# The gate norm's statistics: ten single operations in the first ten attention pairs, or two groups of five in pairs 13 and 14

## The chip, the cores and the metric

The kernel runs on one core of one Trainium2 chip. The metric is the device time of one execution in microseconds, lower is better. The profile is one further execution taken with the hardware profiler, and all times in this text are microseconds from the start of its span unless marked otherwise.

## What is computed

Two layers of a streaming encoder. 512 prompt frames (four tiles of 128 rows) and 8 x 16 new frames of running streams (a fifth tile) go through each layer:

```
xn = RMSNorm(x);  [q|k|v|q_idx|k_idx|w_idx|u|v_s|g_a|g_b] = xn @ W_in
a  = sparse attention: an indexer scores the keys, the best 128 (prompt) or 68 (streams) are kept
s  = gelu(u) * (tril(w_s) @ layer_norm(gelu(v_s)) + b_s)          the spatial gate
h  = x + (sigmoid(g_a) * (a @ W_pa) + sigmoid(g_b) * (s @ W_pb)) @ W_out
y  = h + HierMoE(RMSNorm(h))                                      top group, then two experts
```

The change concerns the `layer_norm` inside `s`, called the gate norm here: per row, the mean and the variance over 512 columns, for five tiles. The outputs of the operator depend on it only through the spatial gate and one returned tensor of normalised rows.

## The kernel before

Every engine has its own program, written out by hand, and the engines meet at semaphores. The part in question is the attention stage of each layer, between the projections of q, k, v, u and those of the two gates. It runs over 20 **pairs** (`NAP`): pairs 0 to 15 are four per prompt tile (`TILE_OF[p]` is `p // 4`), pairs 16 to 19 belong to the streams. A pair is two heads. For pair p:

- PE writes `logits(p)` two pairs ahead (lines 909 to 917), then `probs_transposes(p)` (L929), then a third of a left-over projection of u, `fill(p)` (L776, pairs 0 to 14), then `values(p-1)` (L942 for prompt tiles, L953 and L964 for streams). Before the logits of pair 16, PE waits for `stream_scores`.
- DVE runs, in iteration p of its loop (lines 1700 to 1712): `roots(p)` (the reciprocal L1663, and for the streams the two products L1668, whose two tensor inputs both lie in SBUF); `masked_logits(p+1)` (two L1650 from PSUM, then the small `tensor_scalar` L1658, which makes the exponent's bias of pair p+1 and releases ACT); the selection rounds that `ROUNDS` gives to this iteration (MAX8, MATCH_REPLACE8, L1441; the last ones are in iteration 13, after which `stream_scores` is raised); and, for p below 10, one step of the gate norm's statistics.
- ACT runs `probs_out(p-1)` (L1299), `normalise(p)` (L1289) and `exps(p+1)` (L1283); L1283 waits for L1658 of its pair, L1289 for the `roots` of its pair.

The gate norm itself has three parts. Its statistics are ten DVE operations, `ln_step(0)` to `ln_step(9)` (lines 1628 to 1638): `bn_stats` (L1634) and `bn_aggr` (L1636) for each of the five tiles, each waited for before DVE goes on, since all tiles share one small buffer; the last raises `ln_stat`. POOL waits for `ln_stat`, forms the inverse roots (L539, L542) and normalises in place: five `tensor_scalar` (L636), then ten `tensor_tensor` (L640, five products with the gain and five sums with the bias), one after the other, all 128x512 in SBUF. Each raises `ln_done`. PE's `gating(t)` (L987) waits for `ln_done`; it comes after PE has left the pairs and done its first gate projection, sixteen matmuls of L743. The SP queue waits for the last `ln_done` before it loads the weights of the second half of the gate (a load that also waits for `gating`), and POOL sends the normalised rows out (L643), raises `rows_sent`, and loads the router's weights (lines 648 to 650) after it.

Of the kernel before, what the change touches and what calls it, by code (L numbers as in the profile page):

```python
# [25 lines left out]
NT = PT + 1  # L26
# [98 lines left out]
def prior(name, L):  # L125

    return L * PER_LAYER[name]


SG_BANK = (5, 6, 7, 2, 3)  # L130
PBUF = 4
LBANK = (0, 1, 5, 6)

PROMPT_UNITS = [(t, j, g) for t in range(PT) for j in range(GQ) for g in range(KV)]
# [17 lines left out]
def build(nc, a, o):  # L152
    ctx = ExitStack()
    with ctx:
# [39 lines left out]
        rs_wide = stat[:, 110:110 + NT * (XW - D)].rearrange("p (t c) -> p t c", t=NT)  # L194
        mx, nmx, den, rden = (stat[:, 60 + PBUF * i:60 + PBUF * (i + 1)] for i in range(4))
        moments = stat[:, 18:28].rearrange("p (t c) -> p t c", c=2)
# [25 lines left out]
        q_rep = [scr[:, 512 * g:512 * g + 512] for g in range(KV)]  # L222
        probs = [scr[:, 512 * i:512 * i + 512] for i in range(PBUF)]

        probs_t = [ring[:, VCU % SLOTS, 2048 + 512 * i:2560 + 512 * i] for i in range(PBUF)]
        relu_b = [scr[:, 512 * i:512 * i + 512] for i in range(4)]
# [483 lines left out]
        def _(pe):  # L710
# [22 lines left out]
            for L in range(DEPTH):  # L733
# [168 lines left out]
                def logits(p):  # L902
# [5 lines left out]
                    for n in (2 * p, 2 * p + 1):  # L908
                        t, j, g = ATT_UNITS[n]
                        out = banks[LBANK[n % 4]][:, 0:KEYS[t]]  # L910
                        if t < PT:
# [7 lines left out]
                def probs_transposes(p):  # L919
                    if p == 0:  # L920
                        pe.wait_ge(qts_done, prior("qts_done", L) + 2)
                    for n in (2 * p, 2 * p + 1):
# [5 lines left out]
                        for i, c in enumerate(blocks):  # L928
                            mm = pe.transpose(banks[2 + n % 2][:, i * P:(i + 1) * P],  # L929
                                              probs[n % PBUF][:, c * P:(c + 1) * P], idm)  # L930
                        mm.then_inc(pt_psum, 1)

                def values(p):
# [4 lines left out]
                    if t < PT:  # L938
                        for c in range(t + 1):
                            for h in range(KV):  # L940
                                r = slice(HD * h, HD * h + HD)
                                mm = pe.matmul(banks[4][r, j * P:(j + 1) * P], qkv[:, c, V0 + HD * h:V0 + HD * h + HD],  # L942
                                               probs_t[(2 * p + h) % PBUF][:, c * P:(c + 1) * P],
                                               start=(c == 0), stop=(c == t))
                    else:
# [4 lines left out]
                        for h in range(KV):  # L950
                            r = slice(HD * h, HD * h + HD)
                            o4 = banks[4][r, :].rearrange("p (j q) -> p j q", j=GQ)
                            pe.matmul(o4[:, :, rows], qkv[:, PT, V0 + HD * h:V0 + HD * h + HD],  # L953
                                      probs_t[(2 * p + h) % PBUF][:, 2 * P:3 * P].rearrange("p (j x) -> p j x", j=GQ),
                                      start=True, stop=False)
# [437 lines left out]
        def _(dve):  # L1393
# [3 lines left out]
            def then(ins):  # L1397

                count[0] += 1
                ins.then_inc(dve_chain, 1)  # L1400
                dve.wait_ge(dve_chain, count[0])
# [171 lines left out]
            for L in range(DEPTH):  # L1573
# [47 lines left out]
                def select(t, p):  # L1621

                    begin, rounds = ROUNDS[t]
                    if begin <= p < begin + len(rounds):
                        for r in range(sum(rounds[:p - begin]), sum(rounds[:p - begin + 1])):
                            select_round(t, r)

                def ln_step(i):

                    t, what = divmod(i, 2)  # L1630
                    if i == 0:
                        dve.wait_ge(proj_free, prior("proj_free", L) + 4 * NT)
                    if what == 0:
                        then(V.bn_stats(bns, uv[:, 1, t, :]))  # L1634
                    else:
                        then(V.bn_aggr(moments[:, t, :], bns))  # L1636
                    if i == 2 * NT - 1:
                        V.nop().then_inc(ln_stat, 1)

                def masked_logits(p):  # L1640
                    t, k = TILE_OF[p], 2 * p % PBUF
                    if p and TILE_OF[p - 1] != t:
                        dve.wait_ge(dve_chain, last[t])
                    for h in range(2):
                        n = 2 * p + h
                        dve.wait_ge(s_psum, prior("s_psum", L) + n + 1)
                        if n >= PBUF:
                            dve.wait_ge(pt_psum, prior("pt_psum", L) + n - PBUF + 1)
                        raw = banks[LBANK[n % 4]][:, 0:KEYS[t]]
                        ins = V.tensor_tensor_reduce(out=probs[k + h][:, 0:KEYS[t]], in0=raw,  # L1650
                                                     in1=score(t) if t < PT else zero[:, :].broadcast_to([P, KEYS[PT]]),
                                                     scale=1.0, scalar=NEG, op0=ALU.add, op1=ALU.max,
                                                     accum_out=mx[:, k + h:k + h + 1])
                        if h == 0:
                            ins.then_inc(dve_chain, 1)
                            count[0] += 1
                    then(ins)
                    V.tensor_scalar(nmx[:, k:k + 2], mx[:, k:k + 2], -ATT_SCALE, None, ALU.mult).then_inc(p_raw, 1)  # L1658

                def roots(p):  # L1660
                    t, k = TILE_OF[p], 2 * p % PBUF
                    dve.wait_ge(p_exp, prior("p_exp", L) + 2 * p + 2)
                    ins = V.reciprocal(rden[:, k:k + 2], den[:, k:k + 2])  # L1663
                    if t == PT:

                        then(ins)
                        for h in range(2):
                            ins = V.scalar_tensor_tensor(probs[k + h][:, 3 * P:4 * P].rearrange("p (b i) -> p b i", b=STREAMS),  # L1668
                                                         over(probs[k + h][:, PAST:PAST + FRAMES], STREAMS, 1, [P, STREAMS, FRAMES]),
                                                         rden[:, k + h:k + h + 1],  # L1670
                                                         own_of[:, ATT_UNITS[2 * p + h][1], :].unsqueeze(2).broadcast_to([P, STREAMS, FRAMES]),
                                                         ALU.mult, ALU.mult)
                    ins.then_inc(rden_ready, 1)
# [26 lines left out]
                for p in range(NAP):  # L1700
                    roots(p)
                    if p + 1 < NAP:
                        masked_logits(p + 1)
                    for t in (2, 3, PT):
                        select(t, p)
                    if p == ROUNDS[PT][0] + len(ROUNDS[PT][1]) - 1:
                        dve.wait_ge(dve_chain, last[PT])
                        V.nop().then_inc(stream_scores, 1)
                    if p < 2 * NT:
                        ln_step(p)  # L1710

                for t in range(NT):
                    dve.wait_ge(u_ready, prior("u_ready", L) + t + 1)
# [138 lines left out]
```

## Time and profile before

| | |
|---|---|
| median of 3 runs | 1474.03 us (1470.98 to 1478.52) |
| the profiled execution | 1474.07 us, its span 1472.3 us, mean granted TensorE clock 0.952 |
| PE busy | 1313.5 us, 89% of the span |
| weight loads (PEld) | 727.1 us, 49% |
| DVE busy | 535.8 us, 36% |
| ACT busy | 341.9 us, 23% |
| POOL busy | 222.1 us, 15% |
| chain that ended last | PE 78%, DVE 5%, DMA 5%, issue 4%, ACT 4% |

How to read it: the shares are means over stages with different limits, so the stage of the pairs has to be read by itself, 156 to 257 in the first layer and 872 to 973 in the second. In a timeline a row is the start, the duration, the engine, the line, the operation, output and input with their sizes, how many were merged, and in brackets the idle time before it with what ended it. "Layer 0" and "layer 1" are the first and the second layer.

### The profile page before, as it was taken

What the parts mean: (1) busy time and instruction counts of PE and PEld (TensorE: products, weight loads), DVE (VectorE), ACT (ScalarE), POOL (GpSimd) and SP (SyncE); (2) the same over time, 40 slices, a digit from 0 to 9 for tenths busy, and PEclk for the clock granted to TensorE, in tenths of its full rate; (3) what the DMA queues carried; (4) which work ended last, traced back from release to release, by engine and by line L of the source; (5) the groups of instructions that cost most, each with busy time, mean ns of one, the idle gap of its engine ahead of it and who ended that gap; (6) DMA issues with size and microseconds to landing.
All of it is one profiled execution on the core that took longest, in us unless ns stands there. A gap on an engine that the chain in (4) does not pass through costs nothing.

```text
span 1472.3 us, 15258 instructions
## 1 busy us (share of the span) xinstructions
PE 1313.5 (89%) x5660; PEld 727.1 (49%) x5660; DVE 535.8 (36%) x1502; ACT 341.9 (23%) x773; POOL 222.1 (15%) x304
## 2 busy tenths in 40 slices
PE   7999898999999995988599999899999999879780
PEld 5654345544444454555475544564444445445550
DVE  1278885110111136222335779631101113442115
ACT  2232466100001100222214236541000020112121
POOL 5011033000000001223231200600000000022313
PEclk9999999999999996999799999999999999979895
DMA  8302102503304315899662210051060060369966
GB/s 236 114 13 59 58 1 70 171 1 103 111 0 167 119 51 204 342 405 374 232 150 66 63 57 1 22 180 40 0 214 1 27 244 29 140 244 409 401 230 236
DMA packets 95483, 205.61 MB, mean 140 GB/s; under 512 B 26464, under 2 KB 35904, under 8 KB 95408
## 3 DMA queue, kind: packets, MB, share of 16 engines
q1 hardware_dynamic: 80800, 178.13, 34.2%
q0 software_dynamic: 14608, 26.49, 5.1%
q8 instruction: 46, 0.75, 0.2%
q14 instruction: 29, 0.24, 0.0%
HBM read 196.29 MB, written 27.78 MB: 152 GB/s over the span
## 4 chain that ended last, share of the span: by engine, by line
PE 78%; DVE 5%; DMA 5%; issue 4%; ACT 4%; PEld 1%; PEldq 1%; POOL 1%; SPq 0%; POOLq 0%; ACTq 0%; DVEq 0%
PE bank L743 34%; PE bank L1025 9%; PE bank L1060 9%; PE bank L1106 6%; DMA uv<-xd,mb 3%; PE bank L1117 3%; PE bank L776 3%; PE bank L1093 2%; PE bank L825 1%; DVE stat L1658 1%; PE bank L1042 1%; PE bank L729 1%; PE bank L929 1%; PE bank L829 1%; PE bank L1101 1%
## 5 line engine op out<-in xcount | busy, mean ns | idle before, releaser
L743 PE MATMUL bank<-ring,xt 128*128 128x512 f32 (+1 forms) x1120 | 433.4, 544 | 8.3 <-DMA ring<-in_w_in 5.5
L743 PEld LDWEIGHTS bank<-ring,xt 128*128 128x128 f32 x1120 | 214.2, 194 | 209.5 <-issue 189.2
L1727 DVE TENSOR_TENSOR scr<-scr,bank 128x512 f32<-128x512 f32 x20 | 13.7, 687 | 368.6 <-PE bank L1025 368.6
L1060 PE MATMUL bank<-ring,xt 128*128 128x512 f32 x320 | 141.0, 595 | 0.0
L539 POOL TENSOR_SCALAR stat<-stat 128x1 f32<-128x1 f32 (+1 forms) x27 | 11.3, 418 | 802.8 <-ACT uv L1193 614.3
L1337 ACT ACTIVATE scr<-bank,stat 128x512 f32<-128x512 f32 x40 | 25.3, 683 | 347.9 <-PE bank L743 347.9
L1060 PEld LDWEIGHTS bank<-ring,xt 128*128 128x128 f32 x320 | 59.5, 191 | 67.8 <-issue 67.8
L776 PE MATMUL bank<-ring,xt 128*128 128x512 f32 x160 | 75.4, 605 | 0.0
L1025 PE MATMUL bank<-ring,att 128*128 128x512 f32 x160 | 72.5, 596 | 2.2 <-ACT sgt L1329 1.8
L1025 PE MATMUL bank<-ring,sgt 128*128 128x512 f32 x160 | 71.9, 593 | 0.0
L743 PE MATMUL bank<-more,xt 128*128 128x512 f32 x160 | 70.3, 593 | 0.0
L1762 DVE TENSOR_TENSOR xt<-bank,gain 128x512 f32<-128x512 f32 x68 | 43.8, 686 | 65.8 <-PE bank L1093 65.7
L1106 PE MATMUL bank<-ring,xt 128*64 128x256 f32 x480 | 66.1, 382 | 0.3 <-issue 0.3
L1441 DVE MAX8 stat<-mb 128x8 f32<-128x256 f32 (+3 forms) x114 | 61.6, 540 | 3.0
L1769 DVE SCALAR_TENSOR_TENSOR xt<-bank,uv,xt 128x128 f32<-128x128 f32 x34 | 11.9, 351 | 134.9 <-ACT xt L1358 134.9
L1441 DVE MATCH_REPLACE8 mb<-stat,mb 128x256 f32<-128x256 f32 (+3 forms) x114 | 59.7, 524 | 0.0
L674 POOL DMA_INDIRECT yd<-scr,mb x34 | 34.1, 1002 | 168.4 <-ACT scr L1367 162.7
L1093 PE MATMUL bank<-ident,uv 128*128 128x128 f32 x272 | 41.6, 300 | 18.9 <-DMA uv<-xd,mb 18.9
L1093 PEld LDWEIGHTS bank<-ident,uv 128*128 128x128 f32 x272 | 35.0, 196 | 43.5 <-issue 32.3
L1025 PEld LDWEIGHTS bank<-ring,att 128*128 128x128 f32 x160 | 30.0, 190 | 41.3 <-issue 39.1
L929 PE MATMUL bank<-ident,scr 128*128 128x128 f32 x208 | 35.1, 293 | 16.4 <-ACT scr L1289 16.4
L743 PEld LDWEIGHTS bank<-more,xt 128*128 128x128 f32 x160 | 30.4, 190 | 38.2 <-issue 38.2
(285 smaller groups left out, 1810.0 us busy)
## 6 DMA issues: line engine op xcount, KB each, us to landing
ring<-in_w_in SPq DMA_DIRECT2D x12, 2048.0 KB, 9.2
ring<-in_w_ed SPq DMA_DIRECT2D x32, 512.0 KB, 18.1
ring<-in_w_eg SPq DMA_DIRECT2D x26, 512.0 KB, 10.0
ring<-in_w_eu SPq DMA_DIRECT2D x26, 512.0 KB, 17.1
ring<-in_w_out SPq DMA_DIRECT2D x4, 2048.0 KB, 12.4
more<-in_w_ed SPq DMA_DIRECT2D x14, 512.0 KB, 11.2
qkv<-in_w_eg SPq DMA_DIRECT2D x12, 512.0 KB, 6.7
qkv<-in_w_eu SPq DMA_DIRECT2D x12, 512.0 KB, 8.1
```

What stands on the lines that cost most here:

```text
L674: pool.indirect_dma_start(out=yd, in_=yout[z], in_offset=None, out_offset=bass.IndirectOffsetOnAxis(ap=index(b, 1, q), axis=0), bounds_che ...
L743: mm = pe.matmul(out, xt[:, k, t * P:(t + 1) * P], rhs[:, k, :], start=(k == 0), stop=(k == KD - 1))
L776: mm = pe.matmul(banks[7][:, :], xt[:, k, t * P:(t + 1) * P], rhs[:, k, :], start=(k == 0), stop=(k == KD - 1))
L929: mm = pe.transpose(banks[2 + n % 2][:, i * P:(i + 1) * P], probs[n % PBUF][:, c * P:(c + 1) * P], idm)
L1025: mm = pe.matmul(b[2 + half_][:, :], src[:, j, t * P:(t + 1) * P], w[:, 4 * half_ + j, :], start=(j == 0), stop=(j == 3))
L1060: mm = pe.matmul(banks[5 + n % 3][:, :], xt[:, k, t * P:(t + 1) * P], w[:, k, :], start=(k == 0), stop=(k == KD - 1))
L1093: mm = pe.transpose(banks[first + k // 4][:, (k % 4) * P:(k % 4 + 1) * P], xin[q][:, k:D:KD], idm)
L1106: mm = pe.matmul(banks[2 + z][BR * h:BR * h + BR, 0:2 * P].rearrange("p (m f) -> p m f", m=2), xin_t[z][:, k, BR * h:BR * h + BR], w[:, :, ...
L1117: mm = pe.matmul(banks[4 + c][BR * h:BR * h + BR, :], hidden_t[z][:, BR * h:BR * h + BR], two[h][1][c] if two[h] is places[PLACES - 1] els ...
L1337: ins = act.activation(scr[:, c0:c0 + 512], banks[4 * (n % 2) + m][:, :], ACT.Sigmoid, scale=rs1[:, n % NT:n % NT + 1])
L1441: make(*args, **kwargs).then_inc(dve_chain, 1)
L1762: V.tensor_tensor(xin_t[z][:, 4 * hf:4 * hf + 4, :], banks[first + hf][:, :].rearrange("p (k r) -> p k r", k=4), gain[:, L, 1, 4 * hf:4 * ...
```

## The change

The ten statistics operations are no longer spread one to an iteration over DVE's iterations 0 to 9. The first five (`bn_stats`, `bn_aggr`, `bn_stats`, `bn_aggr`, `bn_stats`) stand at the end of iteration 13, behind the last selection round and behind the raise of `stream_scores`, and the other five at the end of iteration 14, with the raise of `ln_stat` behind the last. What each operation does, and everything on POOL, PE, ACT and SP, is as it was.

```diff
 PBUF = 4
+LN_AT = (13, 14)
 LBANK = (0, 1, 5, 6)
...
                     if p == ROUNDS[PT][0] + len(ROUNDS[PT][1]) - 1:
                         dve.wait_ge(dve_chain, last[PT])
                         V.nop().then_inc(stream_scores, 1)
-                    if p < 2 * NT:
-                        ln_step(p)
+                    if p in LN_AT:
+                        for i in range(NT):
+                            ln_step(NT * LN_AT.index(p) + i)
```

## Rows read from the trace of the kernel before

**Rows 1.** The chain that ended last, both layers: start, us, what.

```profile
221.16 9.83 DVE stat L1658
...
256.56 7.11 PE bank L743 x16
...
935.98 9.30 DVE stat L1658
...
972.52 7.11 PE bank L743 x16
```

**Rows 2.** Timeline of POOL, the gate norm, layers 0 and 1.

```profile
208.36 10.32 POOL L636 TENSOR_SCALAR uv<-uv,stat 128x512 f32<-128x512 f32 x5
218.66 12.31 POOL L640 TENSOR_TENSOR uv<-uv,ring 128x512 f32<-128x512 f32 x10
...
932.95 12.31 POOL L640 TENSOR_TENSOR uv<-uv,ring 128x512 f32<-128x512 f32 x10
```

**Rows 3.** Timeline of DVE, statistics and the operations beside POOL's work, layer 0.

```profile
163.89 0.68 DVE L1634 BATCH_NORM_STATS2 stat<-uv 128x6 f32<-128x512 f32 x1
...
206.35 0.17 DVE L1636 BATCH_NORM_AGGREGATE stat<-stat 128x2 f32<-128x6 f32 x1
...
215.00 0.33 DVE L1658 TENSOR_SCALAR stat<-stat 128x2 f32<-128x2 f32 x1
...
219.81 0.69 DVE L1650 CUSTOM_DVE_ANT_0 scr<-bank,mb 128x512 f32<-128x512 f32 x1
```

**Rows 4.** Timeline of DVE, pairs 15 to 19, layer 0.

```profile
234.04 0.17 DVE L1658 TENSOR_SCALAR stat<-stat 128x2 f32<-128x2 f32 x1
...
244.29 0.61 DVE L1668 SCALAR_TENSOR_TENSOR scr<-scr,stat,own_of 128x128 f32<-128x128 f32 x2
...
245.69 0.17 DVE L1658 TENSOR_SCALAR stat<-stat 128x2 f32<-128x2 f32 x1
...
249.56 0.61 DVE L1668 SCALAR_TENSOR_TENSOR scr<-scr,stat,own_of 128x128 f32<-128x128 f32 x2
...
250.93 0.17 DVE L1658 TENSOR_SCALAR stat<-stat 128x2 f32<-128x2 f32 x1
```

**Rows 5.** Timeline of ACT around the long wait and in pair 18, layer 0.

```profile
223.89 1.34 ACT L1289 ACTIVATE scr<-scr,stat 128x512 f32<-128x512 f32 x2
231.03 0.72 ACT L1283 ACTIVATE scr<-scr,stat 128x512 f32<-128x512 f32 x1 [5.79 <-DVE stat L1658]
...
248.21 0.53 ACT L1283 ACTIVATE scr<-scr,stat 128x272 f32<-128x272 f32 x1
```

**Rows 6.** Timeline of PE, its waits in the pairs, layers 0 and 1.

```profile
173.36 0.62 PE L929 MATMUL bank<-ident,scr 128*128 128x128 f32 x2 [0.80 <-ACT scr L1289]
...
177.97 0.84 PE L929 MATMUL bank<-ident,scr 128*128 128x128 f32 x4 [0.42 <-ACT scr L1289]
...
232.55 0.70 PE L915 MATMUL bank<-qkv,more 128*128 128x272 f32 x2 [3.01 <-DVEq L1708]
...
888.86 0.62 PE L929 MATMUL bank<-ident,scr 128*128 128x128 f32 x2 [0.40 <-ACT scr L1289]
...
946.83 0.70 PE L915 MATMUL bank<-qkv,more 128*128 128x272 f32 x2 [2.47 <-DVEq L1708]
```

**Rows 7.** Timeline of POOL at the start of layer 1, small operations.

```profile
728.83 1.17 POOL L539 TENSOR_SCALAR stat<-stat 128x1 f32<-128x1 f32 x1 [0.83 <-ACT scr L1193]
...
736.25 0.19 POOL L539 TENSOR_SCALAR stat<-stat 128x1 f32<-128x1 f32 x1 [0.86 <-ACT scr L1193]
```

**Rows 8.** PE after its standstill at 712: a 4 us window (busy, granted clock, DMA), then timeline.

```profile
728.00:732.00 4.00, 4.00 (x14) 0.50 1.03 420
```

**Rows 9.** Timeline of PE after the same standstill.

```profile
724.45 1.97 PE L729 MATMUL bank<-ident,x 128*128 128x128 f32 x8 [11.63 <-DVE x L1786]
...
729.44 5.68 PE L743 MATMUL bank<-ring,xt 128*128 128x276 f32 x16
...
735.84 3.89 PE L743 MATMUL bank<-ring,xt 128*128 128x276 f32 x16
```

## Prediction, made before the changed kernel ran

> **What bounds the kernel now.** I read the page's chain by engine first: PE carries most of it, so a DVE change counts only where PE or ACT waits for DVE. Then the chain in order of time, where the stage of the pairs stands out: in each layer one L1658, an operation on two columns, takes 9.83 and 9.30 [rows 1]. That is the bias of pair 14, made in iteration 13. The timeline of POOL says what it waits for. L1658 starts 2.5 after the first L640 and ends at 230.99; the ten L640 end at 218.66 + 12.31 = 230.97. In layer 1 the ends are 945.28 and 945.26 [rows 1, 2]. So DVE stood until POOL's whole row of `tensor_tensor` was over. It is not all of DVE that stands: an L1650, from PSUM, runs in the middle of L640 in its usual 0.69, and an L1658 that falls into L636 takes 0.33 [rows 2, 3].
>
> What did that cost? ACT waited 5.79 for it [rows 5], but PE had work in hand and lost only 3.01 in layer 0 and 2.47 in layer 1, before the logits of pair 16 [rows 6]. The kernel now pays for the collision where five pairs of other work soften it.
>
> **What the change removes.** *Ten DVE steps in iterations 0 to 9.* Five `bn_stats` of 0.68 and five `bn_aggr` of 0.17 [rows 3]. PE waits for DVE in layer 0 twice in these pairs: 0.80 in pair 3, of which 0.40 is ACT's and remains (layer 1 shows that 0.40 without DVE), and 0.42 in pair 4 [rows 6]. So 0.82 is won in layer 0; in layer 1 nothing, as the same two places show no wait for DVE. The bounds are 0 and all ten, 4.3, per layer; I take the waits, since PE sets the pace from pair 5 on.
>
> *The standstill of pair 14.* POOL is idle then, L1658 takes its 0.17, the last selection round follows and `stream_scores` is up before PE asks. PE wins 3.01 and 2.47.
>
> **What it adds.** *Five steps in iteration 13.* About 2.4 of DVE after `stream_scores`. Behind them stand the roots of pair 14, which need ACT's exponentials: ACT ends pair 13's products at 223.89 + 1.34, pipelined at 225.1, and its exponentials take to 226.6. DVE is done near 225.3, so this costs nothing, with 1.3 to spare; without that cover it would be 2.4.
>
> *Five steps in iteration 14.* Exponentials of pair 14 start at 225.1, where they started at 231.03; L1658 of pair 15 came 3.01 after that start [rows 4, 5], so now at 228.1. The last `bn_aggr` starts about 1.95 later (two of 0.68, two of 0.17 and some 0.05 between operations, an estimate): 230.05. Next on DVE are the roots of pair 15, ready at about 230.3: nothing again.
>
> *POOL's work moved.* L640 started 12.31 after the last `bn_aggr` started (206.35 to 218.66) and ends 12.31 later [rows 2, 3]: it now lies from 242.4 to 254.7, and L636 in the ten before it. Gating follows the sixteen L743, which would start at 256.56 - 3.01, so `ln_done` is not itself late. The SP load that also waits for `ln_done` waits for gating too, and the transfers behind it on POOL (rows out, router weights) have hundreds of microseconds: nothing.
>
> **Where it collides.** PE, and ACT behind it, now run 3.01 earlier through pairs 15 to 19 [rows 4]: L1658 of pair 18 comes at 245.69 - 3.01 = 242.7, L1668 of pair 18 at 246.6, L1658 of pair 19 at 247.9. All three lie in L640's stretch, the first by only 0.3. If L1658 of pair 18 stands to 254.7 as pair 14's stood, ACT starts that pair's exponentials at once; from there to L743 it took 256.56 - 248.21 = 8.35 [rows 1, 5]. L743 then starts at 254.68 + 0.04 + 8.35 = 263.07, less 0.82, 262.25: **5.69 later** than 256.56. Nothing softens it here, because no fill and almost no pair is left for PE.
>
> If L1658 gets through by those 0.3, L1668 of pair 18 meets the same stretch. Whether L1668 is held, no row shows directly; the nearest shows the reverse case, POOL's small L539 taking 1.17 where it takes 0.19 with DVE quiet, while DVE runs products with two inputs in SBUF [rows 7]. Then L743 starts 7.00 after the end (249.56 to 256.56), at 261.68 - 0.82: 4.3 later. I take the first case, and the second as nearly the same.
>
> Layer 1 by the same working: the interval from pair 14's L1658 to the end of L640 is 254.68 - 221.16 = 33.52, so 935.98 + 33.52 = 969.50, and L743 at 977.89 against 972.52: **5.37 later** (the 2.47 won is inside this).
>
> *The clock.* PE stands about 9.5 longer before the last two pairs (exponentials of pair 18 at 254.7 instead of 245.2). After a standstill of 11.63 the granted clock was at 0.50, the 1.2 GHz level [rows 8], and sixteen narrow L743 took 5.68 instead of 3.89 [rows 9], 1.8 lost. Bounds 0 and 1.8 plus what the pairs lose; I take 1.2 per layer, because here about six microseconds of pairs 18 and 19 come first and take part of the slow time. 2.4 in all.
>
> **Sum.** 5.69 + 5.37 + 2.4 = 13.5 on the profiled execution's 1474.07, which is the median to 0.04: **1487.5**. After L743 PE sets the pace, so later stages move by the same.
>
> The Trainium skill (SBUF — State Buffer, Who interferes with whom) says that VectorE and GpSimd share a port pair which whoever issues first holds for the whole instruction; `tensor_scalar` and operations with two inputs in SBUF need it. By that, L1658 would have waited for one L640, 1.2, and the trace disagrees: 9.83, which is eight of them.
>
> **Rivals.**
> *One instruction at a time.* If a held DVE operation waits only for POOL's current one, L1658 and L1668 of pair 18 and L1658 of pair 19 each lose at most 1.23 and the L1668 of pairs 16 and 17, beside L636, at most 2.06 [rows 2]: 7.8 per layer, half of it, 3.9, on average. Against 3.83 and 2.47 won that is +0.1 and +1.4: 1475.6. Against it: both L1658 on record waited for the whole row. This is the skill's rule in the same section.
> *Only pair 19 is caught.* If pair 18 slips through and L1668 is never held, L1658 of pair 19 stands to 254.68; from its end to L743 it took 5.46 [rows 1, 4]: 260.14 - 0.82, 2.8 later, and 2.4 in layer 1. With half the clock term 1480.5. For it: the 0.3 is smaller than my errors; against it: rows 7.
> *One step deeper.* If L1668 of pair 17 (241.3) loses 1.1 beside L636, it falls into L640 too and the delay grows by the 1.40 between it and L1658: 1490.3.
> *No collision* (the other side). If DVE gets the port between POOL's operations, or POOL runs enough later that L1658 of pair 19 is out before L640, which takes 5.5, the wins alone stay: 0.82 + 3.01 + 2.47 = 6.3, so 1467.8. For it: the ten steps leave a busy DVE. It decides at one point, whether L1658 of pair 18 is short.
> *That it does not do what it says*, that the steps in iterations 13 and 14 delay the roots: only 1.3 of slack guards pair 14, but the loss is under 1 per layer.
>
> **How the numbers follow.** A stand in pair 18, at L1658 or L1668: 0.56. One deeper: 0.10. Only pair 19: 0.13. One instruction at a time: 0.10. No collision: 0.11. A measurement can tell about 0.5%, 7.4. Slower by more than that are the first two, 0.66; the third, the fourth and half of the last lie within it, 0.28; faster 0.06. The range leaves out no collision and half of the rule below, and the tail of the deeper case above: **1476 to 1493**.
>
> **What would show it.** L1658 with a maximum near 12 at pair 18 and 0.2 at pair 14; no PE wait for `stream_scores`; one wait of PE for L1289 near 10; L636 starting near 231 and L743 near 262 in layer 0. I am wrong if no DVE operation of pairs 18 and 19 ends together with the last L640.

## The result, and the profile after

The changed kernel takes 1483.83 us (median of 10 runs) where the kernel before takes 1475.15 us in the runs beside it; the ratio is 1.0066, with a 95% interval of 1.0045 to 1.0087, so 9.7 us slower (6.6 to 12.8). One of the ten runs of after took 4250.82 us, which nothing on record explains; the ratio leaves it out, and the medians alone lie 8.7 apart. The profiled execution of after took 1484.56 us, with a span of 1482.8 us: 10.5 us more than before's 1472.3. Line numbers of after are one higher than before's.

The chain that ended last (start, us, what) has the standstill in each layer at another place, and longer, than in [rows 1]; the gate's first projection, L744, starts 6.41 later in layer 0 and 12.33 later in layer 1:

```profile
243.03 11.55 DVE stat L1659
...
262.97 7.10 PE bank L744 x16
...
963.45 11.55 DVE stat L1659
...
984.85 7.11 PE bank L744 x16
```

The timeline of DVE in layer 0 says which L1659 it is. Pair 14's, at 220.82, has its 0.17; pair 18's, at 243.03, stands; pair 19's, at 257.32, is short again:

```profile
220.82 0.17 DVE L1659 TENSOR_SCALAR stat<-stat 128x2 f32<-128x2 f32 x1
...
226.41 0.17 DVE L1664 RECIPROCAL stat<-stat 128x2 f32<-128x2 f32 x1 [1.33 <-ACT scr L1284]
...
229.85 0.18 DVE L1637 BATCH_NORM_AGGREGATE stat<-stat 128x2 f32<-128x6 f32 x1
...
243.03 11.54 DVE L1659 TENSOR_SCALAR stat<-stat 128x2 f32<-128x2 f32 x1
...
257.32 0.17 DVE L1659 TENSOR_SCALAR stat<-stat 128x2 f32<-128x2 f32 x1
```

The timeline of POOL shows what it stands for: in layer 0 the ten L641 end at 242.28 + 12.26 = 254.54 and L1659 at 243.03 + 11.54 = 254.57; in layer 1 at 974.96 and 974.99. The rows answer to [rows 2], 23.6 and 29.7 us later than there.

```profile
231.87 10.44 POOL L637 TENSOR_SCALAR uv<-uv,stat 128x512 f32<-128x512 f32 x5
242.28 12.26 POOL L641 TENSOR_TENSOR uv<-uv,ring 128x512 f32<-128x512 f32 x10
...
962.69 12.27 POOL L641 TENSOR_TENSOR uv<-uv,ring 128x512 f32<-128x512 f32 x10
```

ACT's exponentials of pair 18 follow at once (timeline of ACT, first fence), and in the timeline of PE (second fence) the two waits of [rows 6] for the last selection round are gone; in their place PE waits once in each layer for pair 18, and pair 3 keeps the 0.40 that is ACT's:

```profile
254.60 0.52 ACT L1284 ACTIVATE scr<-scr,stat 128x272 f32<-128x272 f32 x1 [9.65 <-DVE stat L1659]
...
975.02 0.52 ACT L1284 ACTIVATE scr<-scr,stat 128x272 f32<-128x272 f32 x1 [9.69 <-DVE stat L1659]
```

```profile
173.70 0.62 PE L930 MATMUL bank<-ident,scr 128*128 128x128 f32 x2 [0.40 <-ACT scr L1290]
...
257.17 1.54 PE L930 MATMUL bank<-ident,scr 128*128 128x128 f32 x6 [10.79 <-ACT scr L1290]
...
977.60 1.54 PE L930 MATMUL bank<-ident,scr 128*128 128x128 f32 x6 [10.84 <-ACT scr L1290]
```

The windows of after around those waits (busy of PE, PEld, DVE, ACT and POOL, then the granted clock, the DMA share and GB/s) show what the standing costs beside the wait itself. The clock is at 0.50, the 1.2 GHz level, when PE comes back, for about 3 us in layer 0; in layer 1 it is still 0.64 on average in the next 4 us. In the kernel before it is 1.00 in the same places (246 to 256.5 and 962 to 972.5).

```profile
246.00:257.00 11.00, 0.39 (x14) 0.25 (x10) 9.78 (x7) 2.27 (x7) 9.20 (x9) 0.68 0.06 25
257.00:260.00 3.00, 2.83 (x26) 2.50 (x26) 1.24 (x6) 2.87 (x10) 2.08 (x3) 0.50 0.13 11
260.00:263.00 3.00, 2.62 (x51) 2.18 (x48) 0.00 (x0) 2.69 (x6) 0.28 (x1) 0.96 0.20 56
...
977.00:981.00 4.00, 3.40 (x28) 2.95 (x29) 1.66 (x8) 3.73 (x10) 2.36 (x3) 0.50 0.17 32
981.00:985.00 4.00, 3.61 (x47) 3.17 (x46) 0.00 (x0) 3.33 (x6) 0.00 (x0) 0.64 0.12 32
```

**A yardstick for the stage.** Single profiles of one kernel differ by several microseconds in stages that no edit touched (shown below), so the stage is also measured by itself: from the last sixteen matmuls of the projections ahead of the pairs to the first gate projection, both in the chain. Before: 151.01 to 256.56 and 865.67 to 972.52, that is 105.55 and 106.85. After: 150.51 to 262.97 and 872.53 to 984.85, 112.46 and 112.32. The change costs the stage 6.9 and 5.5, **12.4 in both**.

### The profile page after: what moved, and what is told of

Same layout as the page of the kernel before. It is cut to its first block, busy times and chain, and to the rows that moved or that the text cites. A ratio compares the mean times of both kernels' runs of the same rounds, so it can differ in the third digit from the quotient of the medians.

```text
span 1482.8 us, 15242 instructions
## 1 busy us (share of the span) xinstructions
PE 1316.8 (89%) x5660; PEld 728.2 (49%) x5660; DVE 541.2 (36%) x1502; ACT 341.0 (23%) x773; POOL 221.3 (15%) x304
## 4 chain that ended last, share of the span: by engine, by line
PE 80%; DVE 5%; DMA 5%; ACT 4%; issue 4%; PEldq 1%; POOL 1%; PEld 0%; POOLq 0%; ACTq 0%; SPq 0%; DVEq 0%
PE bank L744 34%; PE bank L1026 9%; PE bank L1061 9%; PE bank L1107 6%; PE bank L777 4%; DMA uv<-xd,mb 3%; PE bank L1118 3%; PE bank L1094 2%; DVE stat L1659 2%; PE bank L930 2%; PE bank L826 1%; PE bank L1043 1%; DVE x L1788 1%; PE bank L730 1%; PEldq L969 1%
## 5 line engine op out<-in xcount | busy, mean ns | idle before, releaser
L744 PE MATMUL bank<-ring,xt 128*128 128x512 f32 (+1 forms) x1120 | 434.1, 544 | 8.1 <-DMA ring<-in_w_in 5.3
L744 PEld LDWEIGHTS bank<-ring,xt 128*128 128x128 f32 x1120 | 214.3, 194 | 209.9 <-issue 189.6
L777 PE MATMUL bank<-ring,xt 128*128 128x512 f32 x160 | 75.2, 603 | 0.0
L744 PE MATMUL bank<-more,xt 128*128 128x512 f32 x160 | 70.3, 592 | 0.0
L1107 PEld LDWEIGHTS bank<-ring,xt 128*64 128x64 f32 x480 | 40.2, 140 | 19.9 <-issue 4.3
## 6 DMA issues: line engine op xcount, KB each, us to landing
more<-in_w_ed SPq DMA_DIRECT2D x14, 512.0 KB, 10.5
```

Source lines behind the costliest of these rows:

```text
L744: mm = pe.matmul(out, xt[:, k, t * P:(t + 1) * P], rhs[:, k, :], start=(k == 0), stop=(k == KD - 1))
L777: mm = pe.matmul(banks[7][:, :], xt[:, k, t * P:(t + 1) * P], rhs[:, k, :], start=(k == 0), stop=(k == KD - 1))
L1107: mm = pe.matmul(banks[2 + z][BR * h:BR * h + BR, 0:2 * P].rearrange("p (m f) -> p m f", m=2), xin_t[z][:, k, BR * h:BR * h + BR], w[:, :, ...
```

## The experiments

| kernel | median us | ratio to before, 95% | stage, layer 0 / 1 | both, against before |
|---|---|---|---|---|
| before | 1473.3 to 1475.2 | 1 | 105.55 / 106.85 | |
| after | 1483.83 | 1.0066 (1.0045 to 1.0087) | 112.46 / 112.32 | +12.4 |
| e1, after with reduction | 1478.78 | 1.0046 (1.0030 to 1.0063) | 111.20 / 109.72 | +8.5 |
| e2, after with gaps | 1475.34 | 1.0003 (0.9988 to 1.0018) | 107.84 / 106.43 | +1.9 |
| e3, before, late signal | 1480.24 | 1.0057 (1.0035 to 1.0079) | 111.37 / 111.38 | +10.4 |
| e4, groups in 8 and 9 | 1472.77 | 0.9992 (0.9976 to 1.0008) | 107.40 / 106.05 | +1.1 |
| e5, after, half the row | 1472.32 | 1.0001 (0.9982 to 1.0020) | 107.62 / 107.70 | +2.9 |
| e6, after, one column | 1478.67 | 1.0037 (1.0017 to 1.0058) | 111.25 / 106.93 | +5.8 |
| e7, before with reduction | 1467.31 | 0.9966 (0.9947 to 0.9984) | 104.24 / 105.58 | -2.6 |
| e8, before with gaps | 1463.55 | 0.9943 (0.9921 to 0.9964) | 102.51 / 102.17 | -7.7 |
| e9, the same again | 1464.86 | 0.9933 (0.9915 to 0.9951) | 102.53 / 102.65 | -7.2 |
| e10, gaps and reduction | 1466.37 | 0.9944 (0.9924 to 0.9965) | 102.64 / 102.09 | -7.7 |
| e11, groups in 8 and 9, gaps | 1465.24 | 0.9941 (0.9922 to 0.9960) | 103.00 / 104.64 | -4.8 |

The two stage columns come from the chains of the profiled executions, as above. "Before" was run beside each set. From one execution to the next the first fill of a layer, six L776 (L777 with grouped statistics), takes 2.75 or about 4 us (in before the granted clock is 1.00 from 160 to 166 and 0.66 from 876 to 881): the longer time in one layer in most profiles, in both in e3, e5 and e9, in none in e8. With grouped statistics that alone moves the stage of a layer by 1.3 to 1.7, with single ones by 0.6 at most, so the column is to be read with that margin.

### Is it the grouping, or where POOL's work lands? (e3, e4)

e3 is the kernel before, its statistics where they were, with only the signal to POOL late:

```diff
-                    if i == 2 * NT - 1:
-                        V.nop().then_inc(ln_stat, 1)
...
                     if p < 2 * NT:
                         ln_step(p)
+                    if p == 14:
+                        V.nop().then_inc(ln_stat, 1)
```

> The kernel before, statistics one step to an iteration in iterations 0 to 9, with only the raise that starts POOL moved to the end of iteration 14: the move of POOL's work alone. Theory: the move of POOL's work is the loss, the place of the ten operations is worth under 1. POOL starts 2.0 earlier than in the changed kernel, its row ends 2.0 earlier, and the bias of pair 18 stands to that end: the gate projection starts 2 earlier in each layer, and 0.8 later in the first for the ten operations: 1480. Rival (the five operations at a time in iterations 13 and 14 are the loss): close to the kernel before, 1475.

1480.24 us: nearly all of the loss without any grouping. POOL's row lay 1.9 us earlier than in after, and so what stood was not the bias of pair 18 but the products of pair 17, the step that the prediction's deeper rival named. Timelines of POOL and DVE of e3:

```profile
240.41 12.27 POOL L640 TENSOR_TENSOR uv<-uv,ring 128x512 f32<-128x512 f32 x10
```

```profile
241.85 11.24 DVE L1666 SCALAR_TENSOR_TENSOR scr<-scr,stat,own_of 128x128 f32<-128x128 f32 x2
```

They end within 0.41 us of each other (253.09 and 252.68); two products take 0.61 where nothing holds them. e4 is the opposite: grouped, but early.

```diff
-LN_AT = (13, 14)
+LN_AT = (8, 9)
```

> The changed kernel with the two groups of five at the ends of iterations 8 and 9 in place of 13 and 14: POOL starts about where it did in the kernel before, and iterations 0 to 7 are free of the ten operations. Theory: the stand falls on pair 14 again as in the kernel before (9 to 10, of which PE sees 3.0 and 2.5), so the loss is gone; the freed iterations give 0.8 in the first layer at most, and five operations in iterations 8 and 9, where DVE is busy without a pause, cost up to 2 each: 1473 to 1478. Rival (grouping itself costs): 1480 or more.

1472.77 us, just under the range and no difference from before, with the standstill back on pair 14 (timelines of DVE and POOL of e4):

```profile
224.13 9.87 DVE L1659 TENSOR_SCALAR stat<-stat 128x2 f32<-128x2 f32 x1
```

```profile
221.64 12.33 POOL L641 TENSOR_TENSOR uv<-uv,ring 128x512 f32<-128x512 f32 x10
```

So the loss comes with the place of POOL's row, and grouping without that place does not bring it. The groups of e4 are not free all the same: behind the second of them PE waits 1.73 for ACT before the transposes of pair 10, in both layers, which neither before nor after shows (timeline of PE of e4, layer 0). In the whole time it does not show (0.9992).

```profile
210.51 1.05 PE L930 MATMUL bank<-ident,scr 128*128 128x128 f32 x6 [1.73 <-ACT scr L1290]
```

### Which operations stand, and does the row's length set it? (e1, e5, e6)

e1 is the changed kernel with the bias made by a reduction with a minus sign, the scale moved into the masked logits:

```diff
-                    V.tensor_scalar(nmx[:, k:k + 2], mx[:, k:k + 2], -ATT_SCALE, None, ALU.mult).then_inc(p_raw, 1)
+                    V.tensor_reduce(nmx[:, k:k + 2], mx[:, k:k + 2].unsqueeze(2), AX.X, ALU.add, negate=True).then_inc(p_raw, 1)
```

> The changed kernel, with the exponent's bias made by a reduction over one element with the sign turned (the scale 1/8 goes into the masked logits, where it is exact) in place of the small tensor_scalar. Port theory (the tensor_scalar stands because it needs the port that POOL's products use; a reduction does not): no stand at the bias of pair 18 (11.54 in the changed kernel, starting 0.75 into POOL's row). What is late next is the pair of products with two inputs in SBUF in pair 18, some 4 later: if these are held too, they stand to the end of POOL's row near 254.5 and the gate projection starts 1.4 earlier than in the changed kernel in each layer, about 1481. If they are not held, it starts 8 to 9 earlier in each layer, about 1467. Rival (DVE stands for any operation from SBUF to SBUF, or for the tile, not for this form): the reduction stands as long, 1484.

1478.78 us, some 2 us less than was expected of the first case. The reduction, 0.5 into POOL's row, takes 0.15; the products of the same pair, 3.4 us later, stand in its place to the row's end (POOL's row: 243.67 + 12.28 = 255.95). Timeline of DVE of e1:

```profile
244.14 0.15 DVE L1659 TENSOR_REDUCE stat<-stat 128x2 f32<-128x2 f32 x1
...
247.58 8.78 DVE L1669 SCALAR_TENSOR_TENSOR scr<-scr,stat,own_of 128x128 f32<-128x128 f32 x2
```

e5 leaves out the five additions of the norm's bias in each layer (the gate then lacks that bias), which makes the row five long:

```diff
-                for step in range(3):
+                for step in range(2):
...
-                        ins.then_inc(ln_done, 1)
+                        ins.then_inc(ln_done, 1 + step)
```

> The changed kernel without the five additions of the norm's bias in each layer (the gate's input then lacks that bias), so that POOL's row of tensor_tensor has five instructions, some 6.15 us, instead of ten, 12.27. Theory (DVE stands until the whole row is over): the bias tensor_scalar of pair 18 stands some 5.4 us instead of 11.54, ends with the fifth tensor_tensor, and the gate projection starts about 6.1 us earlier in each layer: 1483.8 - 12.3 = 1471.5 us. Rival (one instruction at a time, or another cause of the loss, the grouped statistics themselves): a shorter row changes little, 1480 to 1484 us, since the stand would have the same end.

1472.32 us, as the standstill's theory has it: the bias starts where it did and stands 6.1 us less (timelines of POOL and DVE of e5).

```profile
242.16 6.17 POOL L641 TENSOR_TENSOR uv<-uv,ring 128x512 f32<-128x512 f32 x5
```

```profile
242.91 5.45 DVE L1659 TENSOR_SCALAR stat<-stat 128x2 f32<-128x2 f32 x1
```

e6 makes the bias one column at a time:

```diff
-                    V.tensor_scalar(nmx[:, k:k + 2], mx[:, k:k + 2], -ATT_SCALE, None, ALU.mult).then_inc(p_raw, 1)
+                    for h in range(2):
+                        ins = V.tensor_scalar(nmx[:, k + h:k + h + 1], mx[:, k + h:k + h + 1], -ATT_SCALE, None, ALU.mult)
+                    ins.then_inc(p_raw, 1)
```

> The changed kernel with the bias of a pair made by two tensor_scalars of one column in place of one of two columns. If a tensor_scalar is held whatever its size: the first of the two of pair 18 stands some 11.5 us and the time stays at 1484 us, plus at most 0.1 per pair for the second operation. If the hold comes only with operands of more than one column: no stand at the bias, the products of pair 18 stand instead as in the run with the reduction, and the time is about 1479 us.

1478.67 us, the second answer: a `tensor_scalar` of one column is not held, and the products stand instead. But only in layer 0. In layer 1 the products of the same pair, met by the same kind of row, got through in 2.62 for two (timeline of DVE of e6, layers 0 and 1; POOL's row lies at 243.36 to 255.65 and 963.73 to 976.24). Neither theory had that.

```profile
243.89 0.22 DVE L1660 TENSOR_SCALAR stat<-stat 128x1 f32<-128x1 f32 x2
...
247.21 8.86 DVE L1671 SCALAR_TENSOR_TENSOR scr<-scr,stat,own_of 128x128 f32<-128x128 f32 x2
...
967.49 2.62 DVE L1671 SCALAR_TENSOR_TENSOR scr<-scr,stat,own_of 128x128 f32<-128x128 f32 x2
```

### Gaps in POOL's row, late and early (e2, e7 to e11)

e2 is the changed kernel in which each L641 waits for the one ahead of it, instead of the one five back:

```diff
-                            pool.wait_ge(ln_done, prior("ln_done", L) + NT * (step - 1) + t + 1)
+                            pool.wait_ge(ln_done, prior("ln_done", L) + NT * step + t)
```

> The changed kernel, with each of POOL's ten products and sums waiting for the one before it, so that none is queued behind a running one. Row theory (DVE stands for the whole row because POOL's next operation takes the port before DVE can): with gaps the bias of pair 18 waits for one operation, 1.3 at most, and later ones also one each; POOL's row grows by some 0.1 to 0.3 per operation, and the gate projection starts 6 to 8 earlier in each layer: about 1469 to 1472. Rival (what DVE waits for is the end of the row, or a state that POOL holds from first to last): it stands about 11.5 plus the gaps, 1485 to 1488.

1475.34 us: the whole loss is gone, but not the gain expected. The row grows by 1.2 us; with its gaps the bias of pair 18 waits 0.5, the products of pair 18 1.1, the bias of pair 19 0.3 and its products 2.2 over their 0.17 and 0.61, at the most exposed place. That is 4.1 per layer, 8.2 in all, against the 6.3 that the forecast counts as won. Timeline of DVE of e2:

```profile
244.31 0.66 DVE L1659 TENSOR_SCALAR stat<-stat 128x2 f32<-128x2 f32 x1
...
247.41 1.74 DVE L1669 SCALAR_TENSOR_TENSOR scr<-scr,stat,own_of 128x128 f32<-128x128 f32 x2
...
249.90 0.47 DVE L1659 TENSOR_SCALAR stat<-stat 128x2 f32<-128x2 f32 x1
...
251.76 2.78 DVE L1669 SCALAR_TENSOR_TENSOR scr<-scr,stat,own_of 128x128 f32<-128x128 f32 x2
```

The remaining edits ask whether the kernel before can be rid of its own standstill, pair 14's. e7 is before with e1's reduction, e8 and e9 before with e2's gaps, e10 both, e11 e4 with the gaps.

> The kernel before, with the bias made by a negated reduction (not held by POOL) instead of tensor_scalar. Theory: the stand of pair 14 at the bias (9.83 and 9.30 us) is gone, and PE's waits of 3.01 and 2.47 us for it too, since PE has work in hand while the products of pair 14, held in their turn, wait for the end of the row: 1475 - 5.5 = about 1469 us. Rival (the stand of pair 14 is hidden under the pairs that follow, PE's waits only move): 1475 us.

1467.31 us, 5 us faster (0.16% to 0.53%). The standstill did not vanish: it went to the next operation of that kind, the `tensor_scalar` of 128x272 in the selection round. PE's wait before the logits of pair 16 shrank from 3.01 to 1.51 in layer 0 and from 2.47 to 1.76 in layer 1. Timelines of DVE, POOL and PE of e7:

```profile
219.68 0.16 DVE L1658 TENSOR_REDUCE stat<-stat 128x2 f32<-128x2 f32 x1
...
220.89 8.49 DVE L1441 TENSOR_SCALAR mb<-mb 128x272 f32<-128x272 f32 x1
```

```profile
216.91 12.31 POOL L640 TENSOR_TENSOR uv<-uv,ring 128x512 f32<-128x512 f32 x10
```

```profile
229.58 0.70 PE L915 MATMUL bank<-qkv,more 128*128 128x272 f32 x2 [1.51 <-DVEq L1708]
```

> The kernel before, with each of POOL's tensor_tensor issued only after the one ahead of it is done, so that the row has gaps. Theory: the bias of pair 14 waits for one POOL operation, about 0.7 to 1.3 us, instead of 9.83 and 9.30; its products likewise 1 to 2 us; PE's waits of 3.01 and 2.47 go: 1469 to 1472 us. Rival (the gaps let DVE in only by chance, or the waits add up as in the changed kernel with gaps): 1475 us.

1463.55 us, 8 us faster: better than expected. The bias of pair 14 takes 0.25 and the selection's `tensor_scalar` 0.44 inside the row, and PE does not wait for the last selection round at all (timelines of DVE and POOL of e8):

```profile
221.77 0.25 DVE L1658 TENSOR_SCALAR stat<-stat 128x2 f32<-128x2 f32 x1
...
223.07 0.44 DVE L1441 TENSOR_SCALAR mb<-mb 128x272 f32<-128x272 f32 x1
```

```profile
219.38 13.44 POOL L640 TENSOR_TENSOR uv<-uv,ring 128x512 f32<-128x512 f32 x10
```

> The kernel before with gaps in POOL's row of tensor_tensor, once more and in more runs: 1463 to 1466 us if the gain of about 10 us is its own. Rival: most of the gain was where the granted clock happened to fall in that call, and the median comes back to 1469 to 1472 us.

1464.86 us: the gain is the edit's own. The stage shows why it is more than PE's two waits: it is 3.0 shorter in layer 0, which is the wait of 3.01, but 4.2 (e9) to 4.7 (e8) in layer 1, where the wait was 2.47. In layer 1 of the kernel before the granted clock fell behind that wait (windows of before), while in layer 0 it stayed at 1.00; from the logits of pair 16 to L743 layer 1 then took 972.52 - 946.83 = 25.69, layer 0 24.01. So the standstill of pair 14 cost 1.7 more there than PE's wait shows.

```profile
946.00:950.00 4.00, 3.17 (x12) 2.54 (x13) 2.19 (x8) 4.00 (x11) 0.23 (x1) 0.76 0.17 66
950.00:954.00 4.00, 3.89 (x24) 2.50 (x25) 1.22 (x6) 1.22 (x4) 0.00 (x0) 0.81 0.00 0
```

The two profiles of this one kernel also show how far single profiles are from each other: the spans are 1461.2 and 1468.5, and the same forty matmuls of L1036 in layer 1 take 4.59 in e8 and 6.25 in e9 (chains of e8 and e9).

```profile
1184.94 4.59 PE bank L1036 x40
```

```profile
1187.88 6.25 PE bank L1036 x40
```

> The kernel before with both edits, the gaps in POOL's row and the bias by a negated reduction. With gaps no DVE operation of pairs 13 to 15 waits more than about 1.2 us and PE has work in hand there, so the reduction adds nothing to the gaps: the same as with gaps alone, 1463 to 1466 us. Rival (the waits of about one operation that are left still reach PE): 1 to 3 us faster than with gaps alone.

1466.37 us: nothing on top of the gaps.

> The changed kernel with gaps in POOL's row and the grouped statistics in iterations 8 and 9 in place of 13 and 14, so that POOL's row lies where it lay in the kernel before. If the grouping itself wins the 0.82 us that PE waits for DVE in the first pairs of layer 0, and costs nothing: the same as the kernel before with gaps, to 1 us faster. Rival (five operations at a time delay the roots): 1 to 3 us slower than it.

1465.24 us: by the time, the grouped statistics, placed early, can't be told from the single ones (the two intervals nearly coincide). In the trace the expectation's rival shows: PE waits 1.74 and 1.73 before the transposes of pair 10, as in e4, and the stage gains 4.8 where e8 and e9 gain 7.7 and 7.2. The version to keep is e8's one line.

### The hold by itself (e12)

e12 is the kernel before with 24 rows of ten POOL operations behind all its work, each beside one DVE operation (listed in `PROBES`) whose arrival is shifted by a number of tiny writes:

```diff
+            for r in range(len(PROBES)):
+                pool.wait_ge(ln_stat, DEPTH + r + 1)
+                for i in range(10):
+                    if 10 * r + i >= 5:
+                        pool.wait_ge(ln_done, 3 * NT * DEPTH + 10 * r + i - 4)
+                    v = uv_flat[:, 512 * (i % 5):512 * (i % 5) + 512]
+                    pool.tensor_tensor(v, v, uv_flat[:, 2560:3072], ALU.add).then_inc(ln_done, 1)
...
+            for r, (kind, n) in enumerate(PROBES):
+                V.nop().then_inc(ln_stat, 1)
+                for j in range(n):
+                    ins = V.memset(dst[:, 300 + j:301 + j], 0.0)
+                then(ins)
+                if kind == "product":
+                    ins = V.scalar_tensor_tensor(dst[:, 0:128], src[:, 0:128], src[:, 200:201], src[:, 256:384], ALU.mult, ALU.mult)
+                else:
+                    ins = V.tensor_scalar(dst[:, 0:kind], src[:, 0:kind], 0.5, None, ALU.mult)
```

> The kernel before, with the hold measured by itself behind all its work: 24 times POOL runs ten tensor_tensor of 128x512, one behind the other, and DVE, after a number of tiny memsets that moves its arrival by some 0.2 us from one time to the next, runs one operation: eight times a tensor_scalar of two columns, eight times a product of two 128x128 inputs, four times a tensor_scalar of one column, four times one of 128x272. Theory: two columns, the product and 128x272 stand to the end of the row whatever the phase of their arrival, some 9 to 11 us each; one column never does (0.2 us or less). Rival: the phase of the arrival within POOL's running operation decides, as the one product suggests that got through after 1.3 us in layer 1 of the run with one-column operations, 0.06 us after a POOL operation had begun: then some of the eight with two columns and of the eight products take at most 1.3 us and the others 9 to 11 us. The time as a whole, about 1474 plus 24 times 13 us, 1790 us, tells nothing.

Both were wrong. Of the twenty arrivals of operations that stand in the kernel none stood to the end of its row: two columns took 0.19 to 1.24, the product 0.35 to 1.43, 128x272 0.30 to 1.28, always to about the end of the one POOL operation in progress (L718: 1.26 each). One column took 0.15 four times. In the same execution the kernel's own two rows held the bias of pair 14 for 9.86 and 9.28. From the timeline of DVE of e12, the kernel's own in layer 0, then the shortest and longest of two columns and of the product, and one column:

```profile
221.37 9.86 DVE L1669 TENSOR_SCALAR stat<-stat 128x2 f32<-128x2 f32 x1
...
1523.81 0.19 DVE L1830 TENSOR_SCALAR uv<-uv 128x2 f32<-128x2 f32 x1
...
1548.70 1.24 DVE L1830 TENSOR_SCALAR uv<-uv 128x2 f32<-128x2 f32 x1
...
1585.82 1.43 DVE L1828 SCALAR_TENSOR_TENSOR uv<-uv 128x128 f32<-128x128 f32 x1
...
1622.95 0.35 DVE L1828 SCALAR_TENSOR_TENSOR uv<-uv 128x128 f32<-128x128 f32 x1
...
1659.79 0.15 DVE L1830 TENSOR_SCALAR uv<-uv 128x1 f32<-128x1 f32 x1
```

So POOL's `tensor_tensor` one behind the other are not enough for the long standstill. **What is, stays open.** This row differs from the kernel's in at least five things: each of the kernel's ten operations has two waits in the program, one of which the trace shows as an instruction of its own in POOL's queue (20 for the two layers of after), while here an operation has one wait and only the first of a row has such an instruction (23 for the 24 rows); other engines work meanwhile in the kernel; the kernel's row follows five `tensor_scalar`; its second input lies in another tensor; and DVE's operation here works on the tensor that POOL works on. None of these was tried by itself. Among the rows without gaps inside the kernel, seventeen of eighteen layers held the first such operation to the row's end, in nine profiles (e12's among them); the eighteenth is layer 1 of e6.

## Why the prediction was right, and which sizes were off

1487.5 was forecast and 1483.83 measured; slower by more than 0.5% was given 0.66 and is what came. By its steps:

- **What is removed: the standstill of pair 14.** Right: its bias takes 0.17 and PE's 3.01 and 2.47 before the logits of pair 16 are gone. That it had cost 1.7 of clock besides in layer 1 (see e9) the 2.47 does not hold; the forecast's sum does not suffer, since for layer 1 it starts from the times of before.
- **What is removed: the ten steps, mis-sized.** 0.82 was put down for layer 0 and nothing for layer 1. Up to the transposes of pair 5, where PE waits for ACT in both kernels, the stage takes 32.43 and 32.61 before, 32.61 and 30.96 after, which is 0.18 more in layer 0 and 1.65 less in layer 1, 1.47 less in all (timelines of PE of before, then of after):

```profile
183.44 0.83 PE L929 MATMUL bank<-ident,scr 128*128 128x128 f32 x4 [0.86 <-ACT scr L1289]
...
898.28 0.83 PE L929 MATMUL bank<-ident,scr 128*128 128x128 f32 x4 [0.87 <-ACT scr L1289]
```

```profile
183.12 0.84 PE L930 MATMUL bank<-ident,scr 128*128 128x128 f32 x4 [0.87 <-ACT scr L1290]
...
903.49 0.83 PE L930 MATMUL bank<-ident,scr 128*128 128x128 f32 x4 [0.87 <-ACT scr L1290]
```

It is not the layer that decides but the first fill, which took 2.75 in layer 0 before and in layer 1 after, and 4.30 in the other two. With single statistics a fast fill gains little: 32.43 in layer 0 of e8 with a fast one, 32.44 in e9, the same kernel, with a slow one. The waits of 0.80 and 0.42 in [rows 6] are part of what takes the gain away; e8 has them in layer 0, e9 and e3 do not, with the ten steps in place. With grouped statistics a fast fill gives 30.94 to 30.96 in every profile that has one. So the ten steps cost 1.1 to 1.5 in a layer whose first fill runs at the full clock, and next to nothing in another.

- **Five steps in iteration 13, five in 14.** Right: at no cost, with 1.33 of DVE's idle time left where 1.3 was said; the last `bn_aggr` starts at 229.85, forecast 230.05. Of iterations 8 and 9 it would not have been right (1.73 of PE's time in e4).
- **POOL's row.** 242.28 to 254.54, forecast 242.4 to 254.7.
- **Who is caught.** The likeliest case: L1658 of pair 18, at 243.03 (forecast 242.7), to the end of the row. The margin was small: it came 0.75 after the row had begun. The rivals behind it are real too: with POOL's row 1.9 earlier it is the products of pair 17 (e3), and with the bias out of the way those of pair 18 (e1), which no row of before could show to be held. The reverse case in [rows 7] was read a little too simply: DVE is not quiet at 736.25, where L539 takes 0.19, but runs L1407, whose first input lies in PSUM.
- **The price per layer.** 5.69 and 5.37 forecast, with 1.2 of clock each: 13.5. The stage shows 6.9 and 5.5, 12.4. From the transposes of pair 5 on, where the first fill no longer counts, it is 6.7 and 7.1 longer, where the forecast has 7.7 (5.69 + 0.82 + 1.2) and 6.6 (5.37 + 1.2).
- **The clock, mis-sized too.** From pair 18's exponentials to L744 before took 8.35 and 8.36; after it took 262.97 - 254.60 = 8.37 in layer 0 and 984.85 - 975.02 = 9.83 in layer 1. So the clock did fall to 0.50, but it cost 0.0 and 1.5, not 1.2 and 1.2: in layer 0 it was back at 0.96 from 260 on, in layer 1 only later.
- **"Later stages move by the same."** In the profiled execution they did not: 12.4 in the stage, 10.5 at the end. What comes behind layer 1's pairs took 499.78 before and 497.95 after, and nearly all of that is one group of forty matmuls (6.25 before, 4.59 after); the same group in layer 0 went the other way. e8 and e9 are one kernel and differ in that very group by as much, so this is no effect that the profiles let one lay to the change. By the ratio the whole is 6.6 to 12.8: it holds the stage's 12.4, and the forecast's 13.5 lies just above it. Both mis-sized terms made the forecast too high.

What was too coarse is the mechanism behind the right number. The prediction took "POOL's whole row is waited for" as the law and set the Trainium skill's rule (SBUF — State Buffer, Who interferes with whom: the engine that issues first keeps the shared port pair for that instruction) aside as a rival. In the changed kernel the trace is with the prediction, 11.54 in both layers. With gaps (0.25 to 1.12 for a bias in e2, e8 and e9) and in the row by itself (e12, at most 1.43) it is with the Trainium skill's rule. The rival of one instruction at a time, which had 3.9 per layer and 1475.6, is what e2 brought about: 4.1 per layer and 1475.34. The same section of the Trainium skill says that reductions never contend and that operations with two inputs in SBUF do; e1 agrees, with 0.15 and 8.78.

## What to carry to other kernels

Moving the producer of a POOL job moves the job too, and with it the stretch in which DVE's `tensor_scalar` and two-input operations stand: before such a move, lay POOL's row beside DVE's timeline at the new place, and look how much work PE has in hand there. In the middle of the pairs PE waited 3.01 and 2.47 for the standstill, at their end 10.79 and 10.84. Where POOL's operations must run beside DVE's, let each wait for the one ahead of it: a row 1.1 us longer made the kernel before 0.6% to 0.7% faster (e8, e9), and took the whole loss out of the changed one (e2). That holds for a place where PE has work in hand; at the end of the pairs the short waits still added up to 4.1 per layer.

## What was not expected of the hardware

- A `tensor_scalar` of one column was not held by POOL's row (0.15 each in e12, 0.22 for two in e6), one of two columns was (11.54 in after).
- Taking the held operation away does not take the hold away: it went to the next operation of that kind (e1, 8.78; e7, 8.49).
- A row of POOL operations held DVE for up to 11.54 us in the kernel and never for more than 1.43 in a row by itself, and once (e6, layer 1) not in the kernel either. What decides is open.
